# Two-layer streaming encoder: the mLSTM mixer rewritten from a chunk recurrence to a whole-prompt quadratic form, with its events reordered

## The chip, the cores and the metric

The kernel is one launch on one core of a Trainium2 chip. The metric is device time in microseconds, the median of several runs; less is better. A profiled execution gives the trace that all rows below come from. TensorE is called PE (its weight loads PEld), VectorE DVE, ScalarE ACT, GpSimd POOL, and SP is the engine that issues the weight DMAs.

## The reference, cut to what matters

A prompt of 256 frames and a sample of 64 frames with cached state (320 columns in all, T in the code) go through two layers. Layer 0 is attention, layer 1 is an mLSTM memory; each is followed by a gated convolutional FFN. The change touches the layer 1 mixer only:

```python
bt = jnp.transpose(jnp.cumsum(lf, axis=1), (0, 2, 1))
log_d = jnp.where(causal, bt[..., :, None] - bt[..., None, :] + it[..., None, :], NEG)
log_s = bt + m[..., None]
m_t = jnp.maximum(log_s, jnp.max(log_d, axis=-1))
d = jnp.exp(log_d - m_t[..., None])
s_dec = jnp.exp(log_s - m_t)
w = jnp.einsum('blhk,bshk->bhls', q, k) * d
num = jnp.einsum('bhls,bshv->blhv', w, v) + jnp.einsum('bhl,blhk,bhkv->blhv', s_dec, q, C)
den = jnp.maximum(jnp.abs(den), jnp.exp(-m_t))
...
C_new = sc[..., None, None] * C + jnp.einsum('bhs,bshk,bshv->bhkv', g, k, v)
```

There are 4 heads with 128-wide q and k and 256-wide v. The reference runs this chunk by chunk (64 frames): four chunks for the prompt, from a state of zero, and one for the sample, from the given state. The result is normalised per head, multiplied by sigmoid(og) and projected. The final states (C, n, m) of both streams are outputs.

## The kernel before, in words

All big products run as units. A unit is one block of 128 output channels: 8 slices of 128 inputs, each with three matmuls over 320 columns (high weight with high activation, high weight with low, low weight with high; lines L657 to L659), so 24 matmuls. Its weights arrive in `raw` by one 512 KB DMA, ACT rounds them to `wh` (L1155, function `hi`), DVE makes the rest `wl` (L1437, `lo`); R = 4 buffers, so the `hi` and `lo` of unit u + 4 are queued on ACT and DVE behind the reading of unit u, and `hi` waits until PE has finished unit u.

Every engine runs its own queue in order, and in the layer 1 input stage all queues follow one list, `recurrent_events()`. It mixes the 24 units of the input projection (`in1`; q, k, v, output gate og) with the small work of the mixer. In the kernel before:

- `narrow` projects the 8 gate rows with 24 matmuls (L755 to L757); DVE and ACT make the log forget gates; `gates`, `sums`, `arow`, `spread` bring them to token layout, sum them in chunks and spread them over 128 rows; `maxima` steps through the five chunk maxima on DVE with small instructions;
- `qk` and `wT` compute and transpose the weights of one 128-token tile for all heads; `ktok` and `vtok` transpose k and v;
- for each head h and each chunk, `add` (L1024) is the product that is added to the state C, `inter` (L1038) is q times the state, and for each tile `intra` (L1046) is the weights times v. DVE updates C after each chunk (L1828), so this is a recurrence through PE, ACT and DVE, five steps a head;
- `norm` (DVE with one POOL power) and `heads` (six transposes back, L721) finish a head, and write an `o_hi`/`o_lo` pair of tiles for the output projection `out1`, whose first six k-slices of two units (`("out", k)`) stand ahead of the last `heads`.

PSUM banks 0 to 3 are handed out in turn by `group_banks()` to units and transposes; a group can start when the group before it in its bank has been read (`bank_free`, from the table `READ`). Banks 4 to 7 are assigned by hand in this stage.

Of the kernel before, what the change touches and what calls it, by code (L numbers as in the profile page):

```python
# [21 lines left out]
P = 128  # L22
# [17 lines left out]
REC_COLS = ([P * j for j in range(8)] + [2056 + P * j for j in range(6)] + [1024 + P * j for j in range(8)]  # L40
            + [2056 + P * j for j in (6, 7)])
CHUNKS = [0, 4, 1, 2, 3]
ROWS = [2, 0, 1]
# [31 lines left out]
def recurrent_events():  # L75


    def halves(i):
        return [("half", i, 0), ("half", i, 1)]

    a, b = halves(5), halves(6)
    out = [("unit", 0), ("unit", 1), ("stats",), ("unit", 2), ("narrow",), ("unit", 3), ("unit", 4), ("gates",),
           a[0], ("sums",), a[1], ("arow",), b[0], ("spread", 0), ("spread", 1), b[1], ("spread", 2), ("unit", 7), ("maxima",), ("unit", 8), ("ktok", 0)]
    out += [("weights",), ("unit", 9), ("ktok", 1), ("unit", 10), ("ktok", 2), ("qk", 0), ("unit", 11), ("wT", 0), ("qk", 1), ("unit", 12), ("wT", 1),
            ("qk", 2), ("unit", 13), ("wT", 2), ("unit", 14), ("unit", 15)]
    out += [("vtok", 0, t) for t in range(3)]
    for h in range(MH):
        a, b = halves(16 + 2 * h), halves(17 + 2 * h)
        out += [a[0], ("add", h, 0), ("inter", h, 0), ("add", h, 1), ("inter", h, 1)]
        out += ([("norm", h - 1)] if h else []) + [("add", h, 2), ("inter", h, 2), ("intra", h, 0), a[1]]  # L90
        out += ([("heads", h - 1)] if h else []) + [("add", h, 3), ("inter", h, 3), ("intra", h, 1), b[0], ("add", h, 4), b[1], ("inter", h, 4)]
        out += [("vtok", h + 1, t) for t in range(3) if h + 1 < MH] + [("intra", h, 2)]
    return out + [("norm", MH - 1)] + [("out", k) for k in range(6)] + [("heads", MH - 1)]

def group_order():
# [15 lines left out]
    for l in range(2):  # L113
        if l:
            for e in recurrent_events():
                if e[0] == "unit" or (e[0] == "half" and e[2] == 0):
                    o.append(("in1", e[1]))
                elif e[0] == "narrow":
                    o.append(("narrow1", 0))
                elif e[0] == "ktok":  # L120
                    o.append(("ktok", e[1]))
                elif e[0] in ("vtok", "intra"):
                    o.append((e[0], 3 * e[1] + e[2]))
                elif e[0] == "heads":
                    o += [("heads", 2 * e[1]), ("heads", 2 * e[1] + 1)]
                elif e == ("out", 0):
                    o += [("out1", 0), ("out1", 1)]
        o += [(f"out{l}", i) for i in range(2, 8)] + [(f"up{l}", i) for i in range(2 * FT)]
# [9 lines left out]
def group_banks():  # L138
# [3 lines left out]
    banks, turn, last, previous = [], 0, {}, []  # L142
    for n, key in enumerate(group_order()):
        b = fixed.get(key)
        if b is None:
            b, turn = turn % 4, turn + 1
# [20 lines left out]
def encoder_step(nc, I, O):  # L167
    ctx = ExitStack()
    with ctx:
# [24 lines left out]
        def scratch(name, shape, dt=F32):  # L194
            n = 4
            for s in shape[1:]:
# [1762 lines left out]
```

## Time and profile before

| | us |
|---|---|
| median of 3 runs (1125.15 to 1126.94) | 1125.46 |
| the profiled execution's own time | 1121.56 |
| its span, first to last instruction | 1119.7 |
| mean granted PE clock | 0.992 of full |
| layer 1 input stage, from the gate projection to the end of the last `heads` | 559.01 to 697.08 |

Busy shares of the span: PE 98%, PEld 94%, DVE 62%, ACT 48%, POOL 23%. The profile page gives busy time, the timeline gives single instructions, and a bracket at a row's end is the idle time ahead of it and the instruction that ended it. A matmul's time in a row is longer than its distance to the next row, since matmuls overlap: prices on PE are read from start to start. A matmul on plain float32 shows as two records (x2 for one matmul); the three-way split matmuls and the transposes show as one.

### The profile page before, as it was taken

What the parts mean: (1) busy time and instruction counts of PE and PEld (TensorE: products, weight loads), DVE (VectorE), ACT (ScalarE), POOL (GpSimd) and SP (SyncE); (2) the same over time, 40 slices, a digit from 0 to 9 for tenths busy, and PEclk for the clock granted to TensorE, in tenths of its full rate; (3) what the DMA queues carried; (4) which work ended last, traced back from release to release, by engine and by line L of the source; (5) the groups of instructions that cost most, each with busy time, mean ns of one, the idle gap of its engine ahead of it and who ended that gap; (6) DMA issues with size and microseconds to landing.
All of it is one profiled execution on the core that took longest, in us unless ns stands there. A gap on an engine that the chain in (4) does not pass through costs nothing.

```text
span 1119.7 us, 20638 instructions
## 1 busy us (share of the span) xinstructions
PE 1096.9 (98%) x7433; PEld 1052.4 (94%) x7433; DVE 688.9 (62%) x1274; ACT 540.5 (48%) x932; POOL 259.0 (23%) x386
## 2 busy tenths in 40 slices
PE   9999989999999999999999999999999999999998
PEld 8799989999999999999989676999999999999997
DVE  5876467777777743336865455387777777533364
ACT  5365554555555533335634543545555555433353
POOL 5500143222333210002403002252223223110020
PEclk9999989999999999999999999999999999999999
DMA  9623343655555555543644314525555555555541
GB/s 232 178 76 91 97 133 89 169 157 156 147 149 149 150 153 151 149 149 94 170 129 117 94 57 89 138 57 169 158 161 150 150 150 150 148 150 150 151 120 48
DMA packets 281543, 150.40 MB, mean 134 GB/s; under 512 B 5528, under 2 KB 278112, under 8 KB 281488
## 3 DMA queue, kind: packets, MB, share of 16 engines
q1 hardware_dynamic: 278832, 144.20, 45.3%
q0 software_dynamic: 2512, 5.40, 2.2%
q8 instruction: 38, 0.62, 0.2%
q14 instruction: 17, 0.14, 0.0%
q10 hardware_dynamic: 144, 0.05, 0.0%
HBM read 145.54 MB, written 4.08 MB: 134 GB/s over the span
## 4 chain that ended last, share of the span: by engine, by line
PE 91%; DVE 6%; ACT 2%; issue 1%; DMA 1%; POOL 0%; SPq 0%; ACTq 0%; DVEq 0%
PE bank L657 26%; PE bank L659 26%; PE bank L658 26%; PE bank L681 2%; DVE wl L1437 1%; PE bank L684 1%; PE bank L1024 1%; DVE hL L1441 1%; PE bank L699 1%; ACT wh L1155 1%; PE bank L1038 1%; DVE xT L1471 1%; PE bank L707 1%; PE bank L721 1%; DVE hidden_lo L1914 1%
## 5 line engine op out<-in xcount | busy, mean ns | idle before, releaser
L1437 DVE TENSOR_TENSOR wl<-raw,wh 128x1024 fp32r<-128x1024 f32 x270 | 334.0, 1237 | 252.7 <-ACT wh L1155 250.7
L657 PE MATMUL bank<-hH,wh 128*128 128x320 f32 x1280 | 400.6, 313 | 1.2 <-DVE mix L1486 0.7
L659 PE MATMUL bank<-hH,wl 128*128 128x320 f32 x1280 | 395.5, 309 | 0.0
L658 PE MATMUL bank<-hL,wh 128*128 128x320 f32 x1280 | 395.4, 309 | 0.0
L1155 ACT ACTIVATE wh<-raw 128x1024 fp32r<-128x1024 f32 x270 | 284.4, 1055 | 196.4 <-PE bank L659 181.7
L657 PEld LDWEIGHTS bank<-hH,wh 128*128 128x128 f32 x1280 | 240.4, 188 | 6.8 <-issue 3.3
L658 PEld LDWEIGHTS bank<-hL,wh 128*128 128x128 f32 x1280 | 240.4, 188 | 0.1
L659 PEld LDWEIGHTS bank<-hH,wl 128*128 128x128 f32 x1280 | 240.3, 188 | 0.0
L657 PE MATMUL bank<-hidden_hi,wh 128*128 128x320 f32 x720 | 224.2, 311 | 1.3 <-DVE hidden_lo L1852 1.2
L658 PE MATMUL bank<-hidden_lo,wh 128*128 128x320 f32 x720 | 223.1, 310 | 0.0
L659 PE MATMUL bank<-hidden_hi,wl 128*128 128x320 f32 x720 | 223.0, 310 | 0.0
L657 PEld LDWEIGHTS bank<-hidden_hi,wh 128*128 128x128 f32 x720 | 135.6, 188 | 2.0 <-DVE hidden_lo L1852 1.3
L658 PEld LDWEIGHTS bank<-hidden_lo,wh 128*128 128x128 f32 x720 | 135.7, 189 | 0.0
L659 PEld LDWEIGHTS bank<-hidden_hi,wl 128*128 128x128 f32 x720 | 135.7, 188 | 0.0
L636 POOL TENSOR_TENSOR fb<-cv,us 128x256 f32<-128x256 f32 x64 | 44.2, 691 | 313.9 <-DVE us L1894 198.4
L404 POOL TENSOR_TENSOR sqb<-sqb 128x320 f32<-128x320 f32 x42 | 43.4, 1034 | 206.3 <-ACT sqb L1378 146.0
L1363 ACT ACTIVATE cv<-cv 128x322 f32<-128x322 f32 x64 | 30.3, 474 | 100.8 <-DVE cv L1889 100.8
L1889 DVE SCALAR_TENSOR_TENSOR cv<-gp,PC,cv 128x322 f32<-128x322 f32 x128 | 70.6, 551 | 7.7
L1367 ACT ACTIVATE hidden_hi<-fb 128x320 f32 (+1 forms) x64 | 30.2, 472 | 79.3 <-POOL cs L640 79.3
L640 POOL COPY cs<-gp 128x4 f32 x64 | 62.9, 983 | 0.0
L1898 DVE TENSOR_TENSOR hidden_lo<-fb,hidden_hi 128x320 f32 (+1 forms) x64 | 31.4, 490 | 44.1 <-ACT hidden_hi L1367 44.1
L1360 ACT ACTIVATE cv<-gp,PC 128x322 f32<-128x322 f32 x64 | 42.2, 659 | 22.6 <-DVE gp L1881 21.6
(372 smaller groups left out, 1115.8 us busy)
## 6 DMA issues: line engine op xcount, KB each, us to landing
raw<-in_w_ffn_up SPq DMA_DIRECT2D x128, 512.0 KB, 4.0
raw<-in_w_ffn_down SPq DMA_DIRECT2D x64, 512.0 KB, 4.0
raw<-in_w_rec_in SPq DMA_DIRECT2D x24, 512.0 KB, 3.9
raw<-in_w_att_in SPq DMA_DIRECT2D x18, 512.0 KB, 5.1
raw<-in_w_ple_gate SPq DMA_DIRECT2D x16, 512.0 KB, 4.1
raw<-in_w_att_out SPq DMA_DIRECT2D x8, 512.0 KB, 3.9
raw<-in_w_rec_out SPq DMA_DIRECT2D x8, 512.0 KB, 4.1
raw<-in_w_ple SPq DMA_DIRECT2D x4, 512.0 KB, 3.5
```

Of the source, the lines that this page charges most:

```text
L404: ops.tensor_tensor(sqb[:, 0, :], sqb[:, 0, :], sqb[:, j, :], ALU.add).then_inc(sem("sq_added"), 1)
L636: g.tensor_tensor(fb[:, s, 0:TP], cv[:, s, 0:TP], us[:, s, 0:TP], ALU.mult)
L640: g.tensor_copy(dst, tail).then_inc(sem(f"f{l}"), 1)
L657: mmul(out, a, rh[:, k, :], start=first, stop=False)
L658: mmul(out, a, rl[:, k, :], start=False, stop=False)
L659: m = mmul(out, b, rh[:, k, :], start=False, stop=last)
L1155: A(wh[:, u % R, :], raw[:, u % R, :], ACT.Copy).then_inc(hi_ready, 1)
L1360: A(cv[:, s, :], gp[:, s, 2:T + 4], ACT.Identity, scale=PC[:, l, bass.ds(j + 64, 1)], bias=PC[:, l, bass.ds(j + 96, 1)]).then_inc(sem(f"cv ...
L1363: A(cv[:, s, :], cv[:, s, :], ACT.Gelu_apprx_tanh).then_inc(sem(f"gelu{l}"), 1)
L1437: V.tensor_tensor(wl[:, u % R, :], raw[:, u % R, :], wh[:, u % R, :].bitcast(F32), ALU.subtract).then_inc(lo_ready, 1)
L1889: V.scalar_tensor_tensor(out=cv[:, s, :], in0=gp[:, s, tap:tap + T + 2], scalar=PC[:, l, bass.ds(j + 32 * tap, 1)], in1=cv[:, s, :], op0=A ...
L1898: V.tensor_tensor(FL[:, bass.ds(j, 1), :].rearrange("p a t -> p (a t)"), fb[:, s, :], FH[:, bass.ds(j, 1), :].rearrange("p a t -> p (a t)" ...
```

## The change: what it does

1. The prompt is treated as one piece: all pairs of 256 tokens, in three tiles of weights (keys 0 to 127 by 256 queries, keys 128 to 255 by 128 queries, and the sample's 64 by 64), 448 columns a head, computed already transposed (`W`), so `wT`, `add`, `inter` and `intra` go. `Y` multiplies them with v: five matmuls a head. One matmul a head adds to the sample's state (`Cs`), two make the prompt's (`Cp`).
2. Running sums and maxima are scans along a row on DVE (`running_rows`) instead of chunk steps. The scanned maximum `mu` is split in a high and a low part (`NM`) and spread over 128 rows with a 36-row matmul each head (`spread`). `rows` transposes the gate rows with three small matmuls.
3. The gate projection has one 100-column weight (`wide`) and 16 matmuls instead of 24 (`narrow_wide`).
4. The units stand in another order (`REC_UNITS`), no unit is split in halves, and the small work stands at other places. The last `heads` comes after two output slices instead of six. Banks 4 to 7 are handed out in turn to `rows`, `spread`, `W`, `Y`, `Cs` and `Cp`.
5. POOL's memsets and the three state loads move ahead of the squares of layer 1's input norm (`add_squares(pool, g, "mixpre1")`); POOL scales q for the sample (`q_scaled`) instead of k. One more bias load stands in POOL's first loads.

```diff
 def recurrent_events():
+    e = units(0, 1) + [("stats",)] + units(2) + [("narrow",)] + units(3, 4, 5) + [("rows",), ("spread", 0), ("spread", 1)] + units(6)
+    e += [("spread", 2), ("spread", 3)] + units(7, 8) + [("W", 0), ("ktok", 0)] + units(9) + [("W", 1), ("ktok", 1)] + units(10) + [("vtok", 0)] + units(11)
+    e += [("Y", 0)] + units(12) + [("scale", 0), ("vtok", 1), ("W", 2), ("ktok", 2)] + units(13) + [("Y", 1), ("Cs", 0)] + units(14)
+    e += [("scale", 1), ("heads", 0), ("Cp", 0)] + units(15) + [("W", 3), ("ktok", 3)] + units(16) + [("vtok", 2), ("Cs", 1)] + units(17) + [("Y", 2)] + units(18)
+    e += [("scale", 2), ("heads", 1), ("Cp", 1)] + units(19) + [("Cs", 2), ("Cp", 2)] + units(20) + [("vtok", 3)] + units(21) + [("Y", 3)] + units(22) + [("scale", 3), ("heads", 2)]
+    e += units(23) + [("Cs", 3), ("Cp", 3)]
+    return e + [("out", 0), ("out", 1), ("heads", 3)] + [("out", k) for k in range(2, 6)]
...
 def group_banks():
+    upper = ("rows", "spread", "W", "Y", "Cs", "Cp")
...
+            k = int(key[0] in upper)
+            b = 4 * k + turn[k] % 4
+            turn[k] += 1
...
+            def narrow_wide():
...
+                for k in range(KT):
+                    mmul(out, wide[:, k, :], hH[:, k, :], start=k == 0, stop=False)
+                    m = mmul(out, wide[:, k, :], hL[:, k, :], start=False, stop=k == KT - 1)
...
+                        mmul(gbank(gi)[:, 0:T], selM[:, h:h + 1].to_broadcast([36, P]), NM[:], start=True, stop=True).then_inc(done(gi), 1)
...
+                        mmul(b[:, 0:TP], k[:, 0:P], q[:, 0:TP], start=True, stop=True)
+                        mmul(b[:, TP:TP + P], k[:, P:TP], q[:, P:TP], start=True, stop=True)
+                        mmul(b[0:TS, 384:448], k[:, TP:T], q[:, TP:T], start=True, stop=True).then_inc(done(gi), 1)
...
+                        terms = [[(Pm[:, b, 0:P], Vaug[:, h, 0, :])],
+                                 [(Pm[:, b, P:TP], Vaug[:, h, 0, :]), (Pm[:, b, TP:TP + P], Vaug[:, h, 1, :])],
+                                 [(Pm[0:TS, b, 384:448], Vaug[0:TS, h, 2, :]), (mix[:, h, TP:T], C[:, h, :])]]
...
+            def running_rows():
...
+                dve.wait_ge(sem("lf_ln"), 2)
...
+                for c, n in ((0, TP), (TP, TS)):
+                    V.tensor_tensor_scan(out=Brow[:, c:c + n], data0=one.to_broadcast([4, n]), data1=lf1[:, c:c + n], initial=0.0,
+                                         op0=ALU.mult, op1=ALU.add).then_inc(step, 1)
...
                         if i == 3:
+                            running_rows()
+                        if i == 4:
+                            dve.wait_ge(sem("mu_hi"), 1)
+                            V.scalar_tensor_tensor(out=NM[32:36, :], in0=mu, scalar=-1.0, in1=NM[0:4, :].bitcast(F32),
+                                                   op0=ALU.mult, op1=ALU.subtract).then_inc(sem("mu_split"), 1)
```

How the instructions stand now is shown at three places. The first is PE's queue behind the first halves of head work. Before, at head 0 (`Vaug` is v by tokens with a column of ones, `C` the state, `wT` the weights, `Ktok_92` the weighted k):

```order
L1038 MATMUL bank<-C,mix 64x257 [waits ld_state,C_init]
L1024 MATMUL bank<-Vaug,Ktok_92 128x257
L1038 MATMUL bank<-C,mix 64x257
L1024 MATMUL bank<-Vaug,Ktok_92 128x257 [waits C_new]
L1038 MATMUL bank<-C,mix 64x257 [waits C_new,inter_read]
L1046 MATMUL bank<-Vaug,wT 64x257 [waits mwT_read,vtok_read]
L657 MATMUL bank<-hH,wh 128x320
```

Now, at head 1, between units 13 and 14 (`Pm` is a head's weights, `Kg` its weighted k, `mix` q):

```order
L1041 MATMUL bank<-Vaug,Pm 128x257 [waits Yn]
L1041 MATMUL bank<-Vaug,Pm 128x257
L1041 MATMUL bank<-Vaug,Pm 64x257 [waits ld_state,q_scaled,Yn]
L1041 MATMUL bank<-C,mix 64x257
L1048 MATMUL bank<-Vaug,Kg 128x257 [waits Kg,P]
L665 MATMUL bank<-hH,wh 128x320 [waits lo_ready,vtok_read]
```

Seven matmuls of one half of a head stood there and six of that head's thirteen followed; now five finish the head's output and one its sample state, and the first ones of each bank wait for `P` (the weights from DVE) and `Yn` (a head scaled out of that bank by DVE).

The second place is the gate chain on ACT and DVE. Before, ACT behind the `hi` of unit 2's event (`mz` holds the gates):

```order
L1268 ACT_TABLE_LOAD
L1268 ACTIVATE mz<-mz 8x320 [waits lf_abs]
L1270 ACT_TABLE_LOAD
L1270 ACTIVATE mz<-mz,cst 8x320 [waits lf_exp]
L1155 ACTIVATE wh<-raw 128x1024 [waits unit_used,raw_landed3]
L1155 ACTIVATE wh<-raw 128x1024 [waits unit_used,raw_landed0]
```

Now, behind the `hi` of unit 3's event (`fb` holds the forget gates, `cv` the running rows):

```order
L1278 ACT_TABLE_LOAD
L1278 ACTIVATE fb<-fb 4x320 [waits lf_abs]
L1280 ACT_TABLE_LOAD
L1280 ACTIVATE fb<-fb,cst 4x320 [waits lf_exp]
L1161 ACTIVATE wh<-raw 128x1024 [waits unit_used,raw_landed0]
L1283 ACTIVATE NM<-cv 4x320 [waits mu_ready]
L1161 ACTIVATE wh<-raw 128x1024 [waits unit_used,raw_landed1]
```

DVE before, behind the `lo` of unit 3's event:

```order
L1784 TENSOR_TENSOR mz<-mz 8x320 [waits narrow_step1,lf_ln]
L1486 SCALAR_TENSOR_TENSOR mix<-bank,rstd 128x320 [waits unit_used]
L1437 TENSOR_TENSOR wl<-raw,wh 128x1024 [waits hi_ready]
L1797 COPY gates_tok<-bank 128x32 [waits C_init,mgates_tr]
L1798 COPY gates_tok<-bank 64x16
L1799 COPY ml_lf<-gates_tok 128x12 [waits m_step]
L1802 COPY ml_bt<-bank 128x12 [waits msums]
```

And DVE now, behind the same (`fb`, `cv`, `G` and `NM` have 4 rows):

```order
L1722 TENSOR_TENSOR fb<-fb 4x320 [waits narrow_step1,lf_ln]
L1725 SCALAR_TENSOR_TENSOR cv<-cst,fb 4x256 [waits m_step]
L1725 SCALAR_TENSOR_TENSOR cv<-cst,fb 4x64
L1729 SCALAR_TENSOR_TENSOR G<-us,bcol,cv 4x320 [waits M_init,m_step]
L1732 SCALAR_TENSOR_TENSOR cv<-cst,G 4x256 [waits m_step]
L1732 SCALAR_TENSOR_TENSOR cv<-cst,bcol,G 4x64
L1736 TENSOR_TENSOR G<-cv 4x320 [waits mu_ready]
L1502 SCALAR_TENSOR_TENSOR mix<-bank,rstd 128x320 [waits unit_used]
L1453 TENSOR_TENSOR wl<-raw,wh 128x1024 [waits hi_ready]
L1804 SCALAR_TENSOR_TENSOR NM<-cv,NM 4x320 [waits mu_hi]
L1502 SCALAR_TENSOR_TENSOR mix<-bank,rstd 128x320 [waits unit_used]
```

The exponential and the logarithm moved behind one more `wh`, and DVE's scans, the reading of unit 4 and a `wl` stand ahead of the last step to `NM`, for which PE's `spread` waits (`mu_split`).

The third place is PE behind unit 14: the second half of the transposes of head 0, then the two matmuls of its prompt state `Cp`. Before, such transposes (L721) were followed by an `add` or `intra`:

```order
L721 MATMUL bank<-ident,Y 128x128
L721 MATMUL bank<-ident,Y 128x64
L1024 MATMUL bank<-Vaug,Ktok_92 128x257 [waits C_new]
L1038 MATMUL bank<-C,mix 64x257 [waits C_new,inter_read]
L1046 MATMUL bank<-Vaug,wT 128x257 [waits mwT_read,in_read1]
L657 MATMUL bank<-hH,wh 128x320 [waits lo_ready,Y]
```

Now:

```order
L729 MATMUL bank<-ident,Y 128x128
L729 MATMUL bank<-ident,Y 128x64
L966 MATMUL bank<-Vaug,Kg 128x257 [waits vtok_read,Kg,Yn]
L966 MATMUL bank<-Vaug,Kg 128x257
L665 MATMUL bank<-hH,wh 128x320 [waits lo_ready,in_read1]
```

The first `Cp` matmul waits for `Yn` to reach 4, which is the first tile of head 1, since the bank that it gets (7) held that tile. DVE scales it in the event `("scale", 1)`, behind the reading and the `lo` of unit 14. Before, `add` and `inter` had two banks each of their own.

## Rows read from the trace of the kernel before

**Rows 1.** The page: the span, and busy time of each engine.

```profile
span 1119.7 us, 20638 instructions
...
PE 1096.9 (98%) x7433; PEld 1052.4 (94%) x7433; DVE 688.9 (62%) x1274; ACT 540.5 (48%) x932; POOL 259.0 (23%) x386
```

**Rows 2.** Stretches: length; busy time (x instructions) by engine; PEclk; DMA share; GB/s.

```profile
158.70:165.50 6.80, 5.65 (x22) 5.46 (x23) 5.06 (x11) 2.30 (x6) 2.69 (x4) 0.50 0.12 36
...
176.00:546.00 370.00, 369.08 (x2523) 368.28 (x2522) 229.36 (x374) 180.33 (x269) 81.27 (x118) 1.00 0.51 146
...
553.50:697.00 143.50, 139.19 (x845) 113.62 (x843) 84.60 (x204) 63.44 (x124) 21.36 (x32) 1.00 0.38 101
...
698.05:701.46 3.41, 3.27 (x13) 2.86 (x12) 0.53 (x1) 2.36 (x5) 0.15 (x1) 0.50 0.20 4
```

**Rows 3.** Timeline of PE: start us, us, engine, line, what; the gate projection begins.

```profile
559.01 0.31 PE L755 MATMUL bank<-hH,wnH 128*8 128x320 f32 x1
```

**Rows 4.** Timeline of PE inside the layer 1 input stage.

```profile
598.41 1.06 PE L993 MATMUL bank<-mix 128*128 128x128 f32 x8
...
599.22 0.39 PE L657 MATMUL bank<-hH,wh 128*128 128x320 f32 x1
...
639.84 0.70 PE L1024 MATMUL bank<-Vaug,Ktok 64*128 64x257 f32 x2
...
641.05 0.70 PE L1024 MATMUL bank<-Vaug,Ktok 64*128 64x257 f32 x2
...
645.89 1.16 PE L721 MATMUL bank<-ident,Y 128*128 128x128 f32 x6
...
646.89 0.65 PE L1024 MATMUL bank<-Vaug,Ktok 64*128 64x257 f32 x2
...
651.06 0.42 PE L657 MATMUL bank<-hH,wh 128*128 128x320 f32 x1
...
651.31 0.31 PE L658 MATMUL bank<-hL,wh 128*128 128x320 f32 x1
...
653.75 0.85 PE L1011 MATMUL bank<-ident,sqb 128*128 128x128 f32 x6
...
654.44 0.60 PE L1046 MATMUL bank<-Vaug,wT 128*128 128x257 f32 x2
```

**Rows 5.** Timeline of PE at the end of the input stage.

```profile
694.70 1.21 PE L721 MATMUL bank<-ident,Y 128*128 128x128 f32 x6 [0.52 <-DVE Y L1766]
...
697.08 0.41 PE L657 MATMUL bank<-hidden_hi,wh 128*128 128x320 f32 x1 [1.17 <-DVE hidden_lo L1852]
```

**Rows 6.** Timelines of DVE and ACT, and the scans of line L1675 (ns min/median/max).

```profile
562.72 0.48 DVE L1484 TENSOR_TENSOR mz<-bank,rstd 8x320 f32<-8x320 f32 x1
...
564.15 0.47 ACT L1268 ACTIVATE mz<-mz 8x320 f32<-8x320 f32 x1 [2.52 <-DVE mz L1501]
...
564.64 1.28 ACT L1270 ACT_TABLE_LOAD   x1
...
565.94 0.56 ACT L1270 ACTIVATE mz<-mz,cst 8x320 f32<-8x320 f32 x1
...
L1675 DVE TENSOR_TENSOR_SCAN cv<-cst,bank x1: 648/648/648, 70.9 to 70.9; 8x256 f32<-8x256 f32 x1
...
L1675 DVE TENSOR_TENSOR_SCAN cv<-cst,cv,us x1: 340/340/340, 71.6 to 71.6; 8x64 f32<-8x64 f32 x1
```

**Rows 7.** Timelines of PE, ACT and DVE around the end of unit 23.

```profile
687.62 0.65 PE L1038 MATMUL bank<-C,mix 128*64 128x257 f32 x2
...
687.79 1.06 ACT L1155 ACTIVATE wh<-raw 128x1024 fp32r<-128x1024 f32 x1 [1.49 <-PE bank L659]
...
688.88 1.23 DVE L1437 TENSOR_TENSOR wl<-raw,wh 128x1024 fp32r<-128x1024 f32 x1 [0.66 <-ACT wh L1155]
...
693.21 1.44 DVE L1766 TENSOR_SCALAR Y<-Y,y_f 128x256 f32<-128x256 f32 x3
```

**Rows 8.** Timeline of POOL ahead of the layer 1 input norm.

```profile
534.26 1.14 POOL L404 TENSOR_TENSOR sqb<-sqb 128x320 f32<-128x320 f32 x1 [14.29 <-ACT sqb L1162]
```

More of the change, by code:

```diff
@@ L75, in recurrent_events, with units @@
 def recurrent_events():
[L78 to L93, printed above, removed]
+    def units(*at):
+        return [("unit", i) for i in at]
+    e = units(0, 1) + [("stats",)] + units(2) + [("narrow",)] + units(3, 4, 5) + [("rows",), ("spread", 0), ("spread", 1)] + units(6)
[5 more added lines that the diff above has]
+    return e + [("out", 0), ("out", 1), ("heads", 3)] + [("out", k) for k in range(2, 6)]
 def group_order():
@@ L115, in group_order @@
             for e in recurrent_events():
-                if e[0] == "unit" or (e[0] == "half" and e[2] == 0):
+                if e[0] == "unit":
                     o.append(("in1", e[1]))
@@ L119, in group_order @@
                     o.append(("narrow1", 0))
[L120 to L125, printed above, removed]
+                elif e[0] in ("rows", "spread", "W", "ktok", "Cs", "Cp"):
+                    o.append((e[0], e[1] if len(e) > 1 else 0))
+                elif e[0] in ("vtok", "heads"):
+                    o += [(e[0], 2 * e[1]), (e[0], 2 * e[1] + 1)]
+                elif e[0] == "Y":
+                    o += [("Y", 3 * e[1] + t) for t in range(3)]
                 elif e == ("out", 0):
                     o += [("out1", 0), ("out1", 1)]
-        o += [(f"out{l}", i) for i in range(2, 8)] + [(f"up{l}", i) for i in range(2 * FT)]
+        o += [(f"out{l}", i) for i in range(2, 8)]
+        o += [(f"up{l}", i) for i in range(2 * FT)]
         o += [(f"down{l}", 0), (f"cs{l}", 0)] + [(f"down{l}", i) for i in range(1, 8)] + [(f"ple{l}", i) for i in range(8)]
@@ L340, in encoder_step @@
                                 ("pt_e", "pt_e", 8), ("pt_o", "pt_o", 8), ("pt_s", "pt_s", 8), ("o", "o_lo0", 8), ("in1", "in_read1", 24),
[L341 to L342 removed]
+                                ("narrow1", "narrow_step1", 1), ("rows", "rows_read", 1), ("spread", "sdec", MH), ("W", "P", MH), ("ktok", "Kg", MH),
+                                ("vtok", "vtok_read", 8), ("Y", "Yn", 12), ("Cs", "C_new", MH), ("Cp", "Cp", MH), ("heads", "mo_f", 8)):
             read_by(name, signal, n)
@@ new lines, in input_recurrent @@
+                        for t, last in enumerate((TP - 1, 383, 447)):
+                            n = TOK[t][1]
+                            ins = A(Kg[0:n, h, t, :], gbank(gi)[0:n, t * P:(t + 1) * P], ACT.Copy, scale=Dm[0:n, h, last:last + 1])
+                        ins.then_inc(sem("Kg"), 1)
+                    elif name == "vtok":
+                        h = a[0]
+                        gi = gid("vtok", 2 * h)
+                        bank_full(act, gi)
+                        A(Vaug[:, h, 0:2, 0:DV], gbank(gi)[:, :].rearrange("p (t c) -> p t c", t=2), ACT.Copy).then_inc(sem("vtok_read"), 1)
+                        gi = gid("vtok", 2 * h + 1)
+                        bank_full(act, gi)
+                        A(Vaug[0:TS, h, 2, 0:DV], gbank(gi)[0:TS, 0:DV], ACT.Copy).then_inc(sem("vtok_read"), 1)
+                    elif name == "Y":
+                        h = a[0]
+                        if h >= 2:
+                            bank_full(act, gid("heads", 2 * (h - 2) + 1))
```

572 lines of the change are left out of this document (267 added, 305 removed).

## The prediction

> **What bounds the kernel now.** I read the page first: PE is busy for 1096.9 of 1119.7 us [rows 1], so only time on PE, or a wait of PE, can change the result. Then the table of stretches. From 176 to 546 us, where nothing but units runs, PE is busy for 369.08 of 370 us with 2523 matmuls, thus one each 0.1466 us, and a unit of 24 takes 3.52 us; neither weights nor engines hold it up there [rows 2]. In the layer 1 input stage PE is nearly as busy (139.19 of 143.5 us), but PEld is busy for only 113.62 [rows 2]: much of PE's time goes to small matmuls. The gain must come from there.
>
> The stretch that the change rewrites runs from the gate projection at 559.01 [rows 3] to 697.08, where PE resumes the output units after the last `heads` [rows 5], 138.1 us. In it stand 21 units (504 matmuls) and 6 output slices of two units (36). These 540 matmuls cost 79.2 us and stay. The other 58.9 us are small work and waits, and this is what is replaced.
>
> **The small work after the change, priced from rows.** All starts are read from row to row.
>
> - Gate projection: 16 matmuls of 320 columns, 2.3 us.
> - `spread`: 4 matmuls of 320 columns, 0.6 us, if they run like the others.
> - Transposes: `vtok` takes 0.69 us for six (653.75 to 654.44), 0.115 each [rows 4]. `ktok` has 12, `vtok` 24, `rows` 3: 39 x 0.115 = 4.5 us. `heads` takes 1.00 for six (645.89 to 646.89) [rows 4], for 24 of them 4.0 us.
> - `W`: four float32 matmuls of 128 columns took 0.81 us (598.41 to 599.22), 0.20 each [rows 4]. 448 columns a head are 3.5 of these: 0.71 us, 2.8 us for four heads.
> - The matmuls of 257 columns: before there are 52 (20 `add`, 20 `inter`, 12 `intra`), after 32 (20 in `Y`, 4 `Cs`, 8 `Cp`). Two of them take 1.21 us now (639.84 to 641.05), 0.605 each [rows 4], and almost each carries a wait. By the 128-column price 257 columns would cost 0.41. The new ones are partly free of waits, since the second of a sum follows the first in the same bank. I take 0.50, between the two ends: 16.0 us (13.1 to 19.4).
> - Each change between unit and small work costs some 0.2 us: the first unit matmul after a piece holds the next for 0.25 instead of 0.15 us (651.06, 651.31) [rows 4], and I estimate as much again on the way in. There are 19 such pieces: 3.8 us.
>
> The sum is 34.0 us (31.1 to 37.4), so the work falls by **24.9 us** (21.5 to 27.8). This includes the waits of 0.52 and 1.17 us around the last `heads` [rows 5]: four output slices, 3.5 us, now cover its way through DVE and ACT, which took 2.38 us from 694.70 to 697.08.
>
> **New wait 1, at `rows` and `spread`.** The gate chain starts at the end of the gate projection, now 561.35. ACT copies three rows (some 0.45 each), DVE makes seven small operations of about 0.45 (the first of before took 0.48 [rows 6]), until 566. Meanwhile unit 3 ends at 564.87, and ACT makes a `wh` of 1.06 [rows 7] ahead of the exponential. Then follow a table load 1.28, the exponential 0.47, a load 1.28 and the logarithm 0.56 [rows 6]: 569.6. On DVE: a subtraction 0.45, scans 0.65 and 0.34 [rows 6], a row operation 0.48, scans again, a sum 0.45: `rows_ready` at about 573.05. Then DVE reads unit 4 (0.49) and makes a `wl` (1.23 [rows 7]) before the last operation on `NM`: `mu_split` at 575.2. PE ends unit 5 at 561.35 + 3 x 3.52 = 571.9. It waits until 575.25, less 0.35 us of transposes inside: **3.0 us**. If every DVE step overlapped by 0.1 it would be 1.5 us; with 0.2 us for each of some ten semaphores it would be 5. What stands behind the wait on PE, unit 6, has its weights since long; behind it on DVE stand the reading of unit 5 and a `wl` for unit 9, three units early, so nothing else becomes late.
>
> **New wait 2, at the first `Cp`.** It needs the bank of head 1's first tile. After a unit ends, ACT takes until +1.15 us for `wh` and DVE until +2.4 for `wl` (687.62, 687.79, 688.88 with 1.23) [rows 7]; then the factor 0.17 and a scaling of a third of 1.44 [rows 7]: +3.0. PE has only the transposes of head 0 to do, 1.0 us. **2.1 us** of wait (0 if DVE were idle earlier, 3 at most). I followed the same queues for the other `Y`, `Cs`, `Cp` and `vtok`: at each of them the bank's reader is a whole unit (3.5 us) or more ahead.
>
> **The granted clock.** In 698.05 to 701.46 PEclk is 0.50, which is 1.2 instead of 2.4 GHz [rows 2], just after the two waits around the last `heads` [rows 5]; 13 matmuls in 3.41 us instead of 23 is a loss of some 1.8 us. With these waits gone I expect this one not to come: 1.8 us gained. But new wait 1 is longer than both, so I expect such a stretch behind it: 1.7 us lost. A second behind new wait 2 is left to the range.
>
> **At no cost.** POOL's memsets and state loads, some 7 us of its time (estimated), fall in its idle 14.29 us before 534.26 [rows 8]; were POOL not idle there, they would delay the input norm's squares and with them PE one for one. One more bias load on POOL in the prologue: 0 to 0.8 us, hidden by the units ahead of its reader. DMA traffic of weights is the same, and 146 GB/s fed PE without a pause [rows 2].
>
> **The page that speaks against.** The Trainium skill (ScalarE: Activation LUTs, What ACT_TABLE_LOAD costs) counts about 2.66 us for a switch of function tables, the load and a drain of 1.38. The logarithm's load starts at 564.64 for 1.28 us and its ACTIVATE stands at 565.94 [rows 6], so here there is no drain behind it. With the page's figure for both switches new wait 1 would be 5.8 us and the result 2.8 us later; the trace decides, and the sum goes by the row.
>
> **Sum.** -24.9 + 3.0 + 2.1 - 1.8 + 1.7 = -19.9 us. The profiled execution took 1121.56 us, so the changed one should take about 1101.7 in the profile. The median of before, 1125.46, lies 3.9 us above its profiled execution, and I carry that over: **1105.5 us**.
>
> **The rivals.**
>
> *The waits cost more than two places* (the forecast's mechanism, with the clock against it). Stretches at 0.50 lasted 3.41 us once and 6.80 us once (158.70) [rows 2]. If both new waits bring one of 6.8 us, 6.8 us are lost instead of 1.7, and with the wait 1 at 5 us the result is 1105.5 + 5.1 + 2.0 = 1112.6. For it: waits of 1.7 us together [rows 5] were followed by such a stretch, and mine are 3.0 and 2.1. Against: the stage before had waits of 0.5 to 0.8 us and kept full clock (PEclk 1.00 from 553.5 to 697 [rows 2]).
> The Trainium skill (TensorE: Matmul & The Clock Gate, HAM oscillation) says the same of idle gaps between bursts, that each brings the half rate back, and the trace agrees at 698.05.
>
> *Everything goes well*: 257-column matmuls at 0.41, wait 1 at 1.5 us, no stretch at half clock: 1105.5 - 2.9 - 1.5 - 1.7 = 1099.4, and 1097.3 without wait 2.
>
> *The other side: the shared upper banks hold PE up throughout.* 29 groups go through four banks, and their readers are DVE and ACT in strict order. If a wait like number 2 (2.1 us) stood at ten more of the 20 places of `Y`, `Cs` and `Cp`, the gain would be gone; with eleven the result is 1105.5 + 23.1 = 1128.6. For it: DVE's `head_norm` waits for the squares of all three tiles and holds the unit reads behind it. Against: those reads are needed a unit later at the earliest, and DVE is busy for 84.6 of 143.5 us in the stage [rows 2].
>
> *The change does not do what it says*: the work leaves PE, but the chain from q, k and v to weights and output is what takes the time, and PE waits for it instead. The waits would have to reach 25 us, while each of the four chains has three or more units (10 us) of other work beside it. Result within 0.2% of before, 1125.5.
>
> **Chances.** Forecast, 1100 to 1111: 0.70. More waits and half clock, 1111 to 1122: 0.12. Everything well, under 1100: 0.12. No change: 0.02. Slower: 0.04. The range 1098 to 1113 leaves out the last two, most of the second beyond 1113 and the little under 1098: some 0.15. 0.2% (2.3 us) is about what a measurement of this kernel can tell. Faster 0.94, same 0.02, slower 0.04.
>
> **What would show it.** Right: about 16 gate-projection matmuls and 32 of 257 columns in this stage, 0.45 to 0.55 us apart; PE idle some 3 us ahead of the first `spread`, released by the DVE operation on `NM`; some 2 us ahead of the first `Cp`, released by the scaling of `Y`; no idle time around the last `heads`; the stretch from the gate projection to the end of the last output slices shorter by 18 to 20 us, and the same times as before outside it. Wrong: PE waiting for `Pm`, `Kg` or `Vaug`; idle time behind each head; a later start of the input stage, which would put the loss on POOL; the price of 257 columns outside 0.41 to 0.61.

## The result and the profile after

| | us |
|---|---|
| before, median (range, n) | 1125.31 (1122.20 to 1126.94, 4) |
| after, median (range, n) | 1105.46 (1104.22 to 1106.54, 4) |
| ratio, 95% interval | 0.9826 (0.9802 to 0.9851) |
| profiled execution, before and after | 1121.56, 1104.22 |

The change makes the kernel 1.7% faster: 19.9 us between the medians, 17.3 us between the two profiled executions.

The page of the changed kernel, against [rows 1]: the span, and the busy time of each engine.

```profile
span 1102.5 us, 20374 instructions
...
PE 1077.7 (98%) x7343; PEld 1047.8 (95%) x7343; DVE 677.7 (61%) x1232; ACT 535.0 (49%) x930; POOL 252.9 (23%) x384
```

PE has 90 instructions and 19.2 us of busy time less, and bounds the kernel as before. Next the stretches of the changed kernel (length; busy time by engine; PEclk; DMA share; GB/s). The first goes from the gate projection to the output units behind the last `heads`, the stretch that was 138.1 us. The next two follow the waits below, the fourth follows the last `heads`.

```profile
559.70:677.76 118.06, 112.81 (x689) 101.50 (x687) 69.70 (x154) 54.15 (x112) 6.23 (x10) 0.97 0.39 104
577.20:580.60 3.40, 3.40 (x15) 3.40 (x14) 2.05 (x7) 2.22 (x9) 0.00 (x0) 0.51 0.97 251
625.00:628.50 3.50, 3.16 (x9) 2.79 (x10) 2.93 (x7) 1.29 (x3) 0.00 (x0) 0.51 0.57 150
...
677.80:700.00 22.20, 21.70 (x147) 21.43 (x147) 7.86 (x9) 11.77 (x20) 8.22 (x10) 1.00 0.86 163
```

The stretch is 118.04 us (559.72 to 677.76) and holds 516 unit matmuls, since two output slices stand ahead of the last `heads` now instead of six. At 0.1466 us these are 75.6 us, which leaves 42.4 us for small work and waits where there were 58.9. Around the last `heads` there is no wait and no half clock any more. Instead there are two new stretches at about 0.50 (1.2 of 2.4 GHz). The waits that stand ahead of them, in PE's timeline (start us, us, engine, line, what, idle before and what ended it), with the `heads` ahead of the second:

```profile
574.15 0.32 PE L988 MATMUL bank<-ident,G 36*128 36x36 f32 x3 [1.37 <-DVE G L1736]
576.27 0.53 PE L996 MATMUL bank<-NM,selM 36*128 36x320 f32 x2 [1.80 <-issue]
...
577.53 0.47 PE L666 MATMUL bank<-hL,wh 128*128 128x320 f32 x1
577.80 0.47 PE L667 MATMUL bank<-hH,wl 128*128 128x320 f32 x1
...
622.12 1.15 PE L729 MATMUL bank<-ident,Y 128*128 128x128 f32 x6
625.34 1.23 PE L966 MATMUL bank<-Vaug,Kg 128*128 128x257 f32 x2 [2.07 <-DVE Y L1785]
...
683.82 0.41 PE L665 MATMUL bank<-hidden_hi,wh 128*128 128x320 f32 x1 [0.51 <-ACT mix L1357]
```

Wait 1 is 1.37 + 1.80 = 3.17 us, at `rows` (L988) and `spread` (L996); wait 2 is 2.07 us, at the first `Cp` (L966), released by the scaling of `Y`. Two unit matmuls at half clock begin 0.27 us apart (577.53, 577.80) where 0.147 is usual. Half of 3.4 us, 1.7, is what each of the two stretches loses; the experiments below give 1.65 each. The last row is a wait for an output bank, 0.5 us, which the trace of before doesn't show.

The gate chain that wait 1 waits for, in ACT's and DVE's timelines:

```profile
565.83 1.06 ACT L1161 ACTIVATE wh<-raw 128x1024 fp32r<-128x1024 f32 x1 [2.27 <-PE bank L667]
566.91 1.28 ACT L1278 ACT_TABLE_LOAD   x1
568.21 0.47 ACT L1278 ACTIVATE fb<-fb 4x320 f32<-4x320 f32 x1
568.70 1.28 ACT L1280 ACT_TABLE_LOAD   x1
569.99 0.56 ACT L1280 ACTIVATE fb<-fb,cst 4x320 f32<-4x320 f32 x1
...
570.58 0.48 DVE L1722 TENSOR_TENSOR fb<-fb 4x320 f32<-4x320 f32 x1 [2.43 <-ACT fb L1280]
571.10 0.86 DVE L1725 TENSOR_TENSOR_SCAN cv<-cst,fb 4x256 f32<-4x256 f32 x2
...
573.52 0.48 DVE L1736 TENSOR_TENSOR G<-cv 4x320 f32<-4x320 f32 x1
574.03 0.49 DVE L1502 SCALAR_TENSOR_TENSOR mix<-bank,rstd 128x320 f32<-128x320 f32 x1
574.44 1.21 DVE L1453 TENSOR_TENSOR wl<-raw,wh 128x1024 fp32r<-128x1024 f32 x1
575.69 0.48 DVE L1804 SCALAR_TENSOR_TENSOR NM<-cv,NM 4x320 fp32r<-4x320 f32 x1
```

`G` is ready at 574.0, and PE's transposes start at 574.15. `NM` stands behind the reading of unit 4 and its `wl` and ends at 576.17, and `spread` starts at 576.27. The "issue" of the row above is thus the wait for `NM`.

### The profile page after: what moved, and what is told of

Same layout as the page of the kernel before. It is cut to its first block, busy times and chain, and to the rows that moved or that the text cites. A ratio compares the mean times of both kernels' runs of the same rounds, so it can differ in the third digit from the quotient of the medians.

```text
span 1102.5 us, 20374 instructions
## 1 busy us (share of the span) xinstructions
PE 1077.7 (98%) x7343; PEld 1047.8 (95%) x7343; DVE 677.7 (61%) x1232; ACT 535.0 (49%) x930; POOL 252.9 (23%) x384
## 4 chain that ended last, share of the span: by engine, by line
PE 89%; DVE 6%; DMA 2%; ACT 1%; issue 1%; POOL 1%; SPq 0%; ACTq 0%; DVEq 0%
PE bank L665 26%; PE bank L666 26%; PE bank L667 26%; PE bank L689 1%; DVE wl L1453 1%; DVE hL L1457 1%; PE bank L692 1%; PE bank L1041 1%; DMA raw<-in_w_att_in 1%; PE bank L707 1%; DVE xT L1487 1%; DMA wnr<-in_w_rec_in 1%; DVE hidden_lo L1916 1%; ACT wh L1161 1%; PE bank L715 1%
```

## The experiments

My theory: the time fell because PE has less small work in this stage, which it pays in full there; the two waits, and a stretch at half clock behind each, give part of that gain back. Rivals: the chain of state updates was what took the time before; the half clock belongs to the small work and not to the waits; a wait that is removed comes back elsewhere. Each kernel was timed in turn with the kernel before, on the same chip as those of its group.

### Taking the waits away

`control` is the changed kernel itself.

> The changed kernel once more, on the chip of the three runs beside it, so that they have a base. Expected: 1103 to 1107 us, and in its trace the same two waits of PE (some 3.2 us ahead of the first spread, some 2.1 us ahead of the first Cp) with a stretch at a granted clock of 0.50 of about 3.4 us behind each.

`cp_later`:

```diff
-    e += [("scale", 1), ("heads", 0), ("Cp", 0)] + units(15) + [("W", 3), ("ktok", 3)] + ...
+    e += [("scale", 1), ("heads", 0)] + units(15) + [("Cp", 0), ("W", 3), ("ktok", 3)] + ...
```

> The first Cp is moved behind unit 15. My theory (the wait for the bank of head 1's first tile is 2.1 us, and the stretch at half clock of 3.4 us behind it, which costs 1.7 us, is there because of the wait): both go, 3.8 us less than the control, and PE then runs at full clock from 581 us to the end of the stage. Rival A (the half-clock stretch comes in any case, since small work with little PE load stands there): the wait goes, the stretch stays, 2.1 us less. Rival B (the wait only moves to the next Cp, Cs or W, because DVE is late for all that follows): no change, and PE idles at another of these.

`rows_later`:

```diff
-    ... + units(3, 4, 5) + [("rows",), ("spread", 0), ("spread", 1)] + units(6)
-    e += [("spread", 2), ("spread", 3)] + units(7, 8) + [("W", 0), ("ktok", 0)] + ...
+    ... + units(3, 4, 5, 6) + [("rows",), ("spread", 0), ("spread", 1)] + units(7)
+    e += [("spread", 2), ("spread", 3)] + units(8) + [("W", 0), ("ktok", 0)] + ...
```

> rows and spread 0 and 1 stand one unit later, behind unit 6, and spread 2 and 3 behind unit 7. My theory (wait 1 is the gate chain through DVE and ACT, 3.2 us late, and the stretch at half clock behind it costs 1.7): a unit of 3.5 us covers it, 3.2 + 1.7 = 4.9 us less than the control. Rival A (the stretch stays): 3.2 us less. Rival B (the chain is late also for what follows: the exponentials of Dm, then Pm, then the first Y, each now one unit less ahead of PE): a new wait ahead of ktok's reader, of Y 0 or of Cs 0, and 0 to 2 us less.

`both_later` has both diffs.

> Both moves together. If the two waits and their stretches are independent: 3.8 + 4.9 = 8.7 us less than the control, some 1096 to 1097 us, and no granted clock under 0.9 between 560 us and the end of the stage. If half-clock stretches come in any case: 5.3 us less. If the removal of one wait makes the other longer (the readers' chains are as late as before, and PE gets there sooner): 5 us or less, with the wait seen in the trace.

| | median us (range, n) | less than control | ratio to before, 95% |
|---|---|---|---|
| control | 1104.80 (1103.40 to 1105.81, 5) | | 0.9838 (0.9819 to 0.9856) |
| cp_later | 1101.00 (1100.45 to 1101.02, 5) | 3.8 | 0.9804 (0.9786 to 0.9821) |
| rows_later | 1099.58 (1098.77 to 1100.45, 5) | 5.2 | 0.9790 (0.9773 to 0.9808) |
| both_later | 1095.68 (1095.46 to 1096.27, 5) | 9.1 | 0.9758 (0.9741 to 0.9776) |

All waits of PE between 562 and 700 us (what, total, times, longest), first of `cp_later`, then of `rows_later`:

```profile
PE bank L996 <- issue: 1.8, 1, 1.8
PE bank L988 <- DVE G L1736: 1.4, 1, 1.4
PE bank L665 <- ACT mix L1357: 0.5, 1, 0.5
```

```profile
PE bank L966 <- DVE Y L1785: 2.1, 1, 2.1
PE bank L665 <- ACT mix L1357: 0.5, 1, 0.5
```

Stretches of `cp_later` and of `rows_later`: for each, the place of the wait that stayed and the place of the one that went.

```profile
577.60:581.00 3.40, 3.40 (x15) 3.40 (x14) 1.39 (x6) 2.67 (x10) 0.00 (x0) 0.50 0.94 257
622.00:632.00 10.00, 10.00 (x66) 9.18 (x64) 7.13 (x14) 4.07 (x8) 0.95 (x1) 1.00 0.34 84
```

```profile
575.00:581.00 6.00, 6.00 (x42) 5.42 (x40) 5.94 (x12) 3.37 (x7) 0.00 (x0) 1.00 0.59 150
620.90:624.20 3.30, 3.30 (x11) 2.94 (x12) 2.47 (x6) 1.20 (x3) 0.00 (x0) 0.50 0.65 159
```

Where the wait is gone, PE runs on through the same small work at 1.00; where it stayed, the stretch at 0.50 stayed. So in these traces the half clock came with the wait, and no wait came back elsewhere. The two moves add up: 3.8 + 5.2 = 9.0 against 9.1.

The traces say the same without the scatter of what lies before and behind. From the first matmul of the gate projection to the first of the output norm (L707) PE takes 145.32 us in the changed kernel (559.72 to 705.04), 141.71 in `cp_later`, 140.54 in `rows_later` and 136.80 in `both_later`. Both moves together take away 8.5 us, of which 5.24 are the waits; the other 3.3 are the two stretches, 1.65 each. `both_later` beats both the changed kernel and the kernel before.

It ran twice more as the base of the groups below.

> The kernel with both moves once more, as the base of the three beside it on the same chip: 1095 to 1097 us, with no wait of PE over 0.6 us between the input norm and the output norm, and no stretch under full clock there.

> The kernel with both moves again, as the base of the two beside it on this chip: 1095 to 1097 us.

It took 1095.66 us (1095.42 to 1096.59, 5; ratio 0.9756, 0.9732 to 0.9781) and 1095.97 us (1095.27 to 1096.06, 5; ratio 0.9753, 0.9731 to 0.9774). The first of these from just ahead of the gate projection to the output units, at full clock, with no wait but the output bank's:

```profile
559.19:675.27 116.08, 115.58 (x730) 104.45 (x728) 70.92 (x157) 55.61 (x117) 10.00 (x14) 1.00 0.45 118
```

### How much wait brings the half clock

`nm_early`, with `Cp` moved and `rows` behind unit 5 as in the changed kernel:

```diff
                         if i == 3:
                             running_rows()
-                        if i == 4:
                             dve.wait_ge(sem("mu_hi"), 1)
                             V.scalar_tensor_tensor(out=NM[32:36, :], ...
```

> Base with Cp moved only; rows and spread stand behind unit 5 again, as in the changed kernel, but DVE does the last operation on NM right behind the gate chain, ahead of the reading of unit 4 and of its wl. If wait 1 was made of the chain (1.4 us up to G) and of the 1.7 us that DVE spends on unit 4 first, some 1.5 us of wait are left: 1.5 us above the base without a stretch at half clock behind it, 3.2 above it with one (so this also tells whether a wait of 1.5 us is enough for the stretch). Rival (the wait ends with something else, such as ACT's copy of NM behind its wh): 3 us of wait left, 4.9 above the base, as the changed kernel would be.

`heads_last`:

```diff
-    return e + [("out", 0), ("out", 1), ("heads", 3)] + [("out", k) for k in range(2, 6)]
+    return e + [("out", k) for k in range(6)] + [("heads", 3)]
```

> Base with the last heads put back behind all six output slices, where it stood before the change. The prediction took 1.2 us of wait and 1.8 us of half clock as removed by the new place. If so: a wait of 1.2 us ahead of the output units of head 3 and a stretch at 0.50 behind it, 2.9 us above the base. If the wait of 1.2 us alone doesn't bring the stretch (before, 0.52 us of waiting stood ahead of it): 1.2 above. Rival (DVE is ready much earlier now, so the place makes no difference): the same as the base.

`rows_sooner`. Its expectation names the base wrongly: the kernel that ran is the changed kernel with this one edit, and without the two moves of `both_later`.

```diff
-    ... + units(3, 4, 5) + [("rows",), ("spread", 0), ("spread", 1)] + units(6)
+    ... + units(3, 4) + [("rows",), ("spread", 0), ("spread", 1)] + units(5, 6)
```

> Base with rows and spread 0 and 1 behind unit 4, two units earlier than the base has them and one earlier than the changed kernel. The gate chain is ready at the same time, so PE waits one unit longer than the 3.2 us of the changed kernel: 6.7 us. It asks how the half clock depends on the wait, which the prediction's second case (6.8 us at half clock behind a longer wait) supposed. With one stretch of 3.4 us behind it: 6.7 + 1.7 = 8.4 us above the base; with 6.8 us at half clock: 10.1; with none: 6.7.

`nm_early` took 1097.88 us (1097.16 to 1100.11, 5), 2.2 above its base `both_again`; `heads_last` 1097.13 (1096.47 to 1097.31, 5), 1.5 above. `rows_sooner` took 1107.94 (1107.00 to 1109.36, 4), 12.0 above its base `both_third`. Of `nm_early` a stretch that begins with its only wait, the 1.37 us ahead of `rows`:

```profile
574.00:580.50 6.50, 6.36 (x41) 5.71 (x42) 5.24 (x12) 4.47 (x12) 0.00 (x0) 1.00 0.55 141
```

Of `heads_last` the wait in PE's timeline, and the stretch from its end:

```profile
674.19 0.41 PE L665 MATMUL bank<-hidden_hi,wh 128*128 128x320 f32 x1 [1.16 <-DVE hidden_lo L1854]
```

```profile
674.00:690.00 16.00, 15.31 (x102) 15.05 (x103) 6.24 (x7) 9.02 (x16) 4.22 (x4) 1.00 0.65 129
```

Of `rows_sooner` wait 1 in PE's timeline, and three stretches: at half clock from the end of its first part on, the same from the end of its second part on, and around wait 2:

```profile
574.65 0.46 PE L988 MATMUL bank<-ident,G 36*128 36x36 f32 x3 [4.89 <-DVE G L1736]
576.77 0.87 PE L996 MATMUL bank<-NM,selM 36*128 36x320 f32 x2 [1.66 <-issue]
```

```profile
574.10:580.50 6.40, 4.19 (x16) 3.77 (x17) 4.12 (x10) 4.34 (x12) 0.00 (x0) 0.50 0.34 84
576.77:580.83 4.06, 4.06 (x14) 3.73 (x15) 1.55 (x6) 2.67 (x10) 0.00 (x0) 0.50 0.54 133
626.00:636.00 10.00, 7.93 (x52) 7.04 (x51) 5.91 (x12) 3.58 (x6) 0.32 (x1) 1.00 0.21 52
```

In `nm_early` the wait for `NM` is gone, as the theory had it (DVE makes `NM` right behind the chain), and the 1.37 us up to `G` are left, with full clock in the profiled execution. Of its five timings three lie at 1097.2 to 1097.9, 1.5 to 2.2 above the base; two lie at 1099.2 and 1100.1, with a mean clock of 0.992 and 0.991 instead of 0.994, as with a stretch at half clock more. So after 1.4 us the stretch seems to come at times. For `heads_last` the 1.2 us of wait are there and no stretch, and 1.5 us is what the time shows. `rows_sooner` waited 4.89 + 1.66 = 6.55 us and was at half clock for 6.8 us, twice as long as in the changed kernel. But this stretch began at 574.0, in the first part of the wait, and also covered the second part, in which PE had nothing to do; PE worked at half clock for little more than the 4.06 us of the second row. Its wait 2 is there too, since `Cp` stands in its old place, but this time without a half clock behind it: the last row holds that wait of 2.07 us and has 1.00. From the gate projection to the output norm its trace is 10.9 us longer than that of `both_third` (147.65 against 136.79); less 6.55 and 2.07 of waits that leaves 2.2 us for the half clock, and not 3.4. Another 0.8 us between the two traces is a later start of the gate projection (560.23 against 559.41), which is of the scatter described below. That makes 11.7 for the traces, where the medians have 12.0.

The Trainium skill (TensorE: Matmul & The Clock Gate, HAM oscillation) says that idle gaps between bursts bring the half rate back; the gaps of its example are some 3 to 5 us long. The traces agree for the 3.17 us (three traces of three) and the 6.55. Behind the 2.07 us of wait 2 they show it in three traces of four, so it is a tendency there, not a rule.

### What the small work costs

`y_more`:

```diff
+                            extra = DV + 1 if h % 2 == 0 else DV
+                            for _ in range(3):
+                                mmul(gbank(gi)[0:TOK[t][1], 0:extra], terms[t][0][0], terms[t][0][1][:, 0:extra], start=True, stop=True)
                             for i, (weights, values) in enumerate(terms[t]):
                                 m = mmul(gbank(gi)[0:TOK[t][1], 0:DV + 1], weights, values, ...
```

> Base with 36 matmuls more: each of the twelve tiles of Y has its first matmul issued three times more ahead of its own, with 257 columns for heads 0 and 2 and with 256 for heads 1 and 3 (their results are overwritten). The computation is unchanged. It prices the matmul, and tells whether work on PE in this stage costs its whole time, which is the reason given for the gain. If 257 columns cost 0.50 us each, as estimated: 36 x 0.50 = 18 us above the base; at the price of the 128-column matmul, 0.41: 14.8; at 0.605: 21.8. If a matmul of 256 columns is cheaper than one of 257 by its column alone, the two kinds of heads show nearly the same spacing; if the odd count costs more, 0.41 against 0.50. Rival (the chains through DVE and ACT set the time, PE's work lies beside them): well under 10 us above the base.

It took 1111.39 us (1111.05 to 1112.08, 6), 15.7 above `both_again`: 0.437 us for each of the 36. The first tiles of heads 0 and 1 in PE's timeline:

```profile
598.45 1.46 PE L1042 MATMUL bank<-Vaug,Pm 128*128 128x257 f32 x6
599.75 0.60 PE L1044 MATMUL bank<-Vaug,Pm 128*128 128x257 f32 x2
...
614.09 1.46 PE L1042 MATMUL bank<-Vaug,Pm 128*128 128x256 f32 x6
615.39 0.59 PE L1044 MATMUL bank<-Vaug,Pm 128*128 128x257 f32 x2
```

Three more take 1.30 us (598.45 to 599.75, and 614.09 to 615.39), 0.433 each, with 257 columns as with 256. So a float32 matmul of this width costs nearly the 0.41 of the 128-column price, and the odd column nothing. Work added on PE in this stage is paid in full (36 x 0.433 = 15.6). The rival, that the other engines' chains set the time, falls for the kernel with both moves; the changed kernel differs from it only by its two waits.

`fewer_pieces` joins four small pieces to others:

```diff
-    ... + units(7)
-    e += [("spread", 2), ("spread", 3)] + units(8) + [("W", 0), ("ktok", 0)] + units(9) + [("W", 1), ("ktok", 1)] + units(10) + [("vtok", 0)] + ...
+    ... + units(7, 8)
+    e += [("spread", 2), ("spread", 3), ("W", 0), ("ktok", 0)] + units(9, 10) + [("W", 1), ("ktok", 1), ("vtok", 0)] + ...
...
-    e += [("scale", 1), ("heads", 0)] + units(15) + [("Cp", 0), ("W", 3), ("ktok", 3)] + ...
+    e += [("scale", 1)] + units(15) + [("heads", 0), ("Cp", 0), ("W", 3), ("ktok", 3)] + ...
-    ... + units(19) + [("Cs", 2), ("Cp", 2)] + units(20) + [("vtok", 3)] + ...
+    ... + units(19, 20) + [("Cs", 2), ("Cp", 2), ("vtok", 3)] + ...
```

> Base with four places of small work joined to others, nothing else: spread 2 and 3 with W 0, W 1 and ktok 1 with vtok 0, heads 0 with the first Cp, Cs 2 and Cp 2 with vtok 3. The prediction priced each change between unit and small work at 0.2 us. If right: 0.8 us below the base. If the edges cost 0.4 (0.1 to leave a unit and 0.1 to resume it, and as much again for the first semaphore of a piece): 1.6 below. Rival (the edge is no cost of its own): within 0.3 of the base. If a joined piece finds its reader late, PE waits somewhere and it is above the base.

It took 1095.84 us (1095.57 to 1096.10, 5), 0.1 below `both_third`: nothing. In its timeline the second joined piece:

```profile
592.44 0.31 PE L667 MATMUL bank<-hH,wl 128*128 128x320 f32 x1
592.59 0.59 PE L1003 MATMUL bank<-mix 128*128 128x256 f32 x2
...
593.98 0.82 PE L1023 MATMUL bank<-ident,sqb 128*128 128x128 f32 x6
594.55 0.39 PE L665 MATMUL bank<-hH,wh 128*128 128x320 f32 x1
594.78 0.30 PE L666 MATMUL bank<-hL,wh 128*128 128x320 f32 x1
```

From the last unit matmul ahead to the second behind it are 2.34 us, less 0.29 for the two unit matmuls: 2.05. Apart, in the base, the two pieces cost 1.40 and 0.66 by the same reading, 2.06 together. So the edge of a piece is no cost of its own here: going over from one kind of small work to another costs as much as going back to a unit.

`add_narrow` is the kernel before, with the state's update cut to 8 of 257 columns on PE (its outputs for the recurrent state, and what follows from them, are not the reference's):

```diff
-                        mmul(bank[(7, 5)[k % 2]][:, 0:DV + 1], KmT[...], Vaug[r0:r0 + 64, h % 2, t, :],
+                        mmul(bank[(7, 5)[k % 2]][:, DV - 7:DV + 1], KmT[...], Vaug[r0:r0 + 64, h % 2, t, DV - 7:DV + 1],
```

> The kernel before, in which the 20 matmuls of add make 8 of their 257 columns (the other columns of the state's update are left out; every wait, every other instruction and the whole DVE and ACT work stay). It asks whether the matmuls that the change takes away were what took the time before. If PE's work sets the time there, as the prediction took it: 20 times the difference between a matmul of 257 columns (0.43 to 0.60 us) and one of 8 (some 0.1), 6.6 to 10 us below the kernel before. Rival (before, PE waited for the chain C_new to inter, and the gain of the change came from the chain that went away): within 2 us of the kernel before, with PE's waits for C_new grown in the trace.

It took 1116.87 us (1115.42 to 1119.04, 6) against 1123.78 (11): ratio 0.9939 (0.9918 to 0.9960), 6.9 us less. In PE's timeline one `add` and `inter`, and what follows:

```profile
641.63 0.38 PE L1024 MATMUL bank<-Vaug,Ktok 64*128 64x8 f32 x2
641.95 0.65 PE L1038 MATMUL bank<-C,mix 128*64 128x257 f32 x2
642.52 0.39 PE L1024 MATMUL bank<-Vaug,Ktok 64*128 64x8 f32 x2
```

The pair takes 0.89 us (641.63 to 642.52) where it took 1.21 [rows 4]; 20 times the difference of 0.32 is 6.4 us. No wait of PE for `C_new` appeared. The two traces agree: from the gate projection to the output norm `add_narrow` takes 159.79 us and the kernel before 162.86, 3.1 less, and that in spite of 3.4 us lost to a stretch at half clock which the kernel before doesn't have (the last section). The kernel before was bound by PE's work in this stage, and the chain of updates beside it was not what took the time. The expectation had taken 0.1 us for 8 columns, and its range reached just down to what came.

## Why the prediction was right

The time, 1105.46, is the one forecast, 1105.5, and the mechanism came as told: less work on PE, and two new waits at the places named. But that the number fits to 0.1 us is luck: the profiled execution was forecast 2.5 us too low, and the step from there to the median 2.7 us too high.

**The work.** Forecast 34.0 us of small work, so 24.9 less. In the changed kernel 42.4 us less the waits (5.24) and the clock (3.4) leaves 33.8, and 58.9 - 33.8 = 25.1 less. Right, but not by its own terms. Read as above, from the last unit matmul ahead to the second behind, the gate projection takes 2.33 us, `rows` and `spread` 1.5, the four `W` with `ktok` 5.6, `vtok` 2.6, the four `Y` 10.6, `Cs` and `Cp` 6.6, and `heads` 4.8. So the 32 matmuls of 257 columns cost 17.2 us, 0.54 each. One that repeats the weights and the tile costs 0.433; the other 0.1 comes with a change of weights, of tile or of the kind of work, which no run parts. I had 0.50 for each, and 0.2 for each of 19 edges, which joining pieces in `fewer_pieces` doesn't save. The 3.8 us of edges stood for what lies in the operations themselves: by the readings above, 1.4 us more in `W` with `ktok`, 1.2 in the matmuls of 257 columns, 0.8 in `heads` and 0.5 in `rows` and `spread` than I had.

**Wait 1**: 3.0 forecast, 3.17 measured, at the place and by the operations named. **Wait 2**: 2.1 and 2.07. The bounds were wide because a step on a semaphore was unknown; in the chain it is small, from ACT to DVE (569.99 + 0.56, and 570.58) as within DVE (570.58 + 0.48, and 571.10), 0.03 to 0.04 us, so the wait came near neither end. The table load had no drain behind it: 566.91 + 1.28, and the exponential stands at 568.21. The Trainium skill (ScalarE: Activation LUTs, What ACT_TABLE_LOAD costs) counts a drain of 1.38 us at each; the measurement decides. The Trainium skill (ScalarE: Activation LUTs, Table sets: the hidden batching unit) knows a set with both exponential and logarithm; here each had its own load, and no run tries the one.

**The clock.** The stretch at the output units is gone, and one stands behind wait 1 (1.7), as forecast. The first was priced too high: its 13 unit matmuls take 1.9 us at full clock, so of the 3.41 us 1.5 were lost and not 1.8. The step that failed is "a second behind new wait 2 is left to the range": it came, for 1.7 us more. `cp_later` shows that it goes with that wait. Of the 1.2 us that the new place of the last `heads` saves, `heads_last` shows the wait whole; that the half clock at this place also needs the 0.52 us ahead of it is suggested by its absence there, and not shown.

**Outside.** The gate projection starts 0.7 us later than before, at 559.72. Most of this is scatter from the very start of the program: the first transposes of `xtok` stand at 7.58 us in the trace of before and at 8.21 in that of the changed kernel, but at 7.62 in `both_third` and at 8.61 in `add_narrow`, which has the code of before. Another 0.3 us is the change's. It comes at 39 us, where PE waits for DVE's reading of a unit, first before and then after:

```profile
38.42 0.42 PE L657 MATMUL bank<-hH,wh 128*128 128x320 f32 x1 [0.69 <-DVE mix L1486]
```

```profile
39.45 0.41 PE L665 MATMUL bank<-hH,wh 128*128 128x320 f32 x1 [1.01 <-DVE mix L1502]
```

This wait is 0.69 us in both traces with the code of before and 1.00 to 1.06 in all twelve with the code of the change. The bias load that was added on POOL stands shortly ahead of it, which the prediction gave 0 to 0.8 us and took as hidden; that it is the cause is not shown. Some 0.3 us are made up again before 520 us, where the traces are 0.7 apart. POOL's memsets and loads ahead of the squares cost nothing: it was idle for 8.60 us still ahead of its first square, where it had been for 14.29 [rows 8]. Behind the stage the output norm and the units behind it took 0.4 us less. With the output bank's 0.5 the profiled execution comes to -25.1 + 3.17 + 2.07 - 1.5 + 3.4 + 0.7 + 0.5 - 0.4 = -17.2, and it was -17.3, at 1104.22, where 1101.7 was forecast.

**The median.** This is the part that cancelled those 2.5 us. I carried over 3.9 us between median and profiled execution. For the changed kernel it is 1.2, so 2.7 us came in by luck. Over the 31 timings of the kernel before in the three groups the medians are 1123.06, 1123.42 and 1123.78, with single ones from 1120.03 to 1127.27, at a mean clock from 0.995 down to 0.988: the lower the clock, the longer. So what I carried was in the main a draw of half-clock stretches, and not a constant; in a group of its own the changed kernel gains 18.3 us (`control`).

The rivals: a shared upper bank held PE up in one place, not in ten, and none of PE's other waits for `Pm`, `Kg` or `Vaug` appeared.

## What to carry to other kernels

Where PE is busy throughout a stage, count its instructions and price each kind by the distance between starts, not by columns alone; what is taken away there is time, as long as PE waits for none of the chains beside it. Then ask of each small piece put among the big ones when its input is ready, and put it one unit later if that is a wait: each wait of 2 to 3 us mostly cost 1.7 us more in the clock, and moving two pieces by one unit each gained 9.1 us here, about half of what the change itself had brought. A median of few timings carries a draw of such stretches; compare medians with medians and traces with traces, and don't add the difference of one kernel to the other.

## What the hardware showed that I had not expected

- Half clock follows waits by their length only loosely: 1.2 us brought none; 1.4 none in the trace, and by the times perhaps in two of five; 2.07 a stretch of 3.4 us in three traces of four; 3.17 one of 3.4; 6.55 one of 6.8, which began while PE still waited. In `add_narrow` a stretch of 6.8 us, the row below, stood 3 us behind a wait of 0.8 us, at a place where the kernel before had full clock with the same wait.

```profile
581.50:588.10 6.60, 6.60 (x26) 6.04 (x26) 5.79 (x15) 1.06 (x1) 0.00 (x0) 0.50 0.26 66
```

- The stretch behind the output norm, which every kernel here has, was 3.4 us long in the changed kernel's trace and 10 us in that of `control`, the same code. The cost is much smaller than the difference in length, since PE also waits in this place: from the norm's first matmul to that of the next norm it is 20.17 us (705.04 to 725.21) and 20.83 us (704.98 to 725.81), 0.7 us more. First the row of the changed kernel, then that of `control`:

```profile
710.30:713.80 3.50, 3.06 (x11) 3.06 (x12) 3.43 (x6) 2.36 (x7) 2.63 (x3) 0.51 0.00 0
```

```profile
707.20:717.20 10.00, 8.28 (x31) 7.69 (x32) 8.09 (x14) 4.17 (x10) 5.81 (x6) 0.50 0.17 48
```

- The kernel before ranges over 7 us in 31 timings, the changed kernel over 2.4 in the five of `control`, the one with both moves over 1.3 in 15. That the waits make the scatter is not shown: `cp_later`, which has wait 1, ranges over 0.6 in five.
- A float32 matmul costs 0.433 us with 256 columns as with 257. At the place of `add`, where weights change, 257 columns took 0.63 us (639.84 to 640.47 before) and 8 columns 0.32 (641.63 to 641.95 in `add_narrow`), so most of a narrow one is not columns.
